# First feed-forward layer of a hybrid transformer block: weight blocks stationary, 256 token columns moving

## The chip, the cores and the metric

The kernel is one program on one core of a Trainium2 chip. The metric is the device time of the program in microseconds (us), the median of several executions. TensorE (PE in the profile) does the matrix products: it loads a stationary block of up to 128x128 values (a weight load, PEld in the profile) and streams the columns of a moving operand past it, up to 512 for one matmul, the width of one bank of PSUM in float32. PSUM has eight such banks. VectorE (DVE), ScalarE (ACT) and GpSimd (POOL) do the rest, and SyncE (SP) issues most of the loads.

## The reference

One block on 256 tokens of width 2048, all in float32: modulated RMS norm, a fused projection, grouped attention and a Fourier mixing branch, gates, an output projection with a residual, and then the part that matters here:

```python
def sq_relu_mlp(h, w1, w2):
    return jnp.square(jax.nn.relu(h @ w1)) @ w2

h2 = modulate(rmsnorm(x, norm2_g[l]), sh2, sc2)
x = x + g2 * sq_relu_mlp(h2, w1[l], w2[l])
```

`h2` is 256 x 2048, `w1` 2048 x 8192 and `w2` 8192 x 2048.

## The kernel before, in words

**Number format.** Every product is made of three. A float32 operand is split into a high part, the value rounded to float32r, and a low part, the rest. The product is high x high + high x low + low x high, three float32r matmuls that accumulate in PSUM (`products`, L1192 to L1198). Activations are kept as two tiles (`h2T[0]` high, `h2T[1]` low). Weights come as float32 tiles of 128 x 1024 (`raw`, eight slots, 512 KB each); ScalarE makes the high part in `wh` (`split_hi`, L583 to L588), VectorE the low part in `wl` (`split_lo`, L898 to L902). `wh` and `wl` have four slots each, and tile k takes slot k mod 4. ScalarE may write a slot when TensorE has finished the tile that was there (`gemm_done`); VectorE follows ScalarE (`wh_done`), TensorE follows VectorE (`wl_done`), and SyncE loads the next tile into `raw` when VectorE has read the slot.

**Order.** Each engine has a written-out order of its own. After the projections and attention the first feed-forward layer runs over eight blocks i of 1024 features and, in each, over sixteen tiles k of 128 rows of `w1` (`first_product`, L1414). For a tile, `tile_products` (L1200) goes over four banks: bank n holds tokens n mod 2 (128 of them, on partitions) by features n // 2 (512 of them, along columns). The stationary operand is the activation, `h2T[.][:, k, 128 tokens]`, the moving one 512 columns of the weights. So one tile is 4 x 3 = 12 matmuls of 512 columns with 12 weight loads, and all eight blocks use the same banks 0 to 3.

**Behind a block.** VectorE evicts the four banks with a relu into `hs`, tokens on partitions (`relu`, L1102, after the split of tile 1 of the next block). The second layer contracts over features and needs them on partitions, so TensorE transposes `hs` into banks 4 to 7 (`hidden_transposes`, L1421): four groups of four 128x128 transposes, after tiles 1 to 4 of the next block, or behind everything for the last block. ScalarE squares each of these banks into `hid` (`hidden`, L791, after its splits of tiles 3 to 6). `hid` holds all 8192 features by 256 tokens. The blocks 2 to 7 of TensorE are a hardware loop, those of the other engines 1 to 7.

**Around the layer.** In the first block, `xs_transposes` stand between the products: they bring the normalised activations features first, and ScalarE and VectorE make `h2T` from them while the first products run. The second layer (`second_product`, L1452) has the activations stationary again, as two tiles `hidS` that are cut from `hid` (L819 and L1150), and accumulates over all tiles in the eight banks; its tiles alternate between banks 0 to 3 and banks 4 to 7.

Of the kernel before, what the change touches and what calls it, by code (L numbers as in the profile page):

```python
# [21 lines left out]
F32 = mybir.dt.float32  # L22
# [5 lines left out]
P = 128  # L28
# [165 lines left out]
def block_program(nc, x, c, ctx_, c_ctx, w_ada, b_ada, norm1_g, w_in, q_norm_g, k_norm_g,  # L194
                  w_attn_o, w_fourier, w_out, norm2_g, w1, w2, final_norm_g,
                  identity, dft, rope_c, rope_s, out):
    with ExitStack() as stack:
# [10 lines left out]
        def place(name, shape, dt, region, skip=0):  # L208
            return nc.alloc_sbuf_tensor_at(name, shape, dt, offset=where[region] + skip)
# [26 lines left out]
        h2T = [place(f"h2T{i}", [P, KT, T], F32R, "h", i * 16384) for i in range(2)]  # L236
# [28 lines left out]
        hs = place("hs", [P, TB, NC], F32, "f")  # L265
# [65 lines left out]
        def sem(name):  # L331
            return stack.enter_context(nc.semaphore(name))
# [51 lines left out]
        x1_ready = sem("x1_ready")  # L384
        sq1_ready = sem("sq1_ready")
        xs_ready = sem("xs_ready")
        hT_full = sem("hT_full")
        hid_ready = sem("hid_ready")
        hs_hi = sem("hs_hi")
        hs_lo = sem("hs_lo")  # L390
# [170 lines left out]
        def _(act):  # L561
# [210 lines left out]
            def modulate2_hi(g):  # L772
                b = misc_wait_full(act, ("xs", g))
                for j in range(2):
                    f = 2 * g + j
                    nc.scalar.activation(h2T[0][:, f, :], b[:, j * T:(j + 1) * T], ACT.Identity,
                                         bias=mods2[:, 0, f:f + 1], scale=gain2[:, f:f + 1]).then_inc(hi_done, 1)

            for m, (name, k) in enumerate(TILES):
# [10 lines left out]

            def hidden(i, g):  # L791

                act.wait_ge(hT_full, i * 4 + (g + 1))
# [48 lines left out]
        def _(dve):  # L842
# [229 lines left out]
            def modulate2_lo(g):  # L1072
                b = misc_wait_full(dve, ("xs", g))

                dve.wait_ge(hi_done, HI_AT["xs", 2 * g + 1])
                if g >= 2:
                    misc_wait_freed(dve, ("xs", g - 2))
                for j in range(2):
                    f = 2 * g + j
                    then(nc.vector.tensor_scalar(hmod2[:, g % 2, j, :], b[:, j * T:(j + 1) * T], gain2[:, f:f + 1],  # L1080
                                                 mods2[:, 0, f:f + 1], ALU.mult, ALU.add))
                nc.vector.tensor_tensor(h2T[1][:, 2 * g:2 * g + 2, :], hmod2[:, g % 2, :, :],  # L1082
                                        h2T[0][:, 2 * g:2 * g + 2, :].bitcast(F32), ALU.subtract)\
                    .then_inc(misc_free[MISC_AT["xs", g][0]], 1)

            for m, (name, k) in enumerate(TILES):
# [12 lines left out]
            def lo_1(i, k):  # L1099
                split_lo(i * KT + (M1 + k + 1), S1 + k, wh[:, k % SPL, :], wl[:, k % SPL, :])  # L1100

            def relu(i):  # L1102

                for b in range(4):
                    if b < 3:
                        dve.wait_ge(bank_full, i * 3 + (3 * CI1 + b + 1))
                    else:
                        dve.wait_ge(gemm_done, i * KT + (M1 + KT))
                    if b == 0:

                        if not (isinstance(i, int) and i == 0):
                            dve.wait_ge(hT_full, i * 4)
                    nc.vector.tensor_scalar(hs[:, b % 2, b // 2 * HC:(b // 2 + 1) * HC], bank[b][:], 0.0, None, ALU.max)\
                        .then_inc(bank_free, 1)

            for k in range(KT):
                lo_1(0, k)
# [14 lines left out]
                if k in (10, 12):  # L1132
# [7 lines left out]
            with nc.vector.Fori(1, N1) as i:  # L1140
                for k in range(KT):
                    lo_1(i, k)
                    if k == 1:
                        relu(i - 1)

            def lo_2(g, j):
                if j % 4 == 0:
# [6 lines left out]
            for j in range(8):  # L1154
                lo_2(0, j)
                if j == 1:
                    relu(N1 - 1)
# [25 lines left out]
        def _(pe):  # L1183
# [227 lines left out]
                xs_transposes(g)  # L1411
            pe.wait_ge(bank_free, 4 * CI1)

            def first_product(i, k):  # L1414
                pe.wait_ge(wl_done, i * KT + (M1 + k + 1))
                if isinstance(i, int) and i == 0 and k % 2 == 0:
                    misc_wait_freed(pe, ("xs", k // 2))
                tile_products(h2T, k, k % SPL, range(4), k == 0, k == KT - 1,
                              i * 4 + (4 * CI1 - 3) if k == 0 else None)

            def hidden_transposes(i, g):  # L1421

                if g == 0:
                    pe.wait_ge(bank_free, i * 4 + 4 * (CI1 + 1))
                if isinstance(i, int) and i == 0:
                    if g in (1, 2, 3):
                        pe.wait_ge(misc_free[4 + g], _uses[4 + g])
                else:
                    pe.wait_ge(hid_ready, i * 4 + (g - 3))
                for n in range(4):  # L1430
                    f, t = 2 * g + n // 2, n % 2
                    ins = nc.tensor.transpose(bank[4 + g][:, n * P:(n + 1) * P], hs[:, t, f * P:(f + 1) * P], ident[:])  # L1432
                ins.then_inc(hT_full, 1)

            for k in range(KT):
                first_product(0, k)
                if XS_NOW + k < 8:
                    xs_transposes(XS_NOW + k)
            for k in range(KT):
                first_product(1, k)  # L1440
                if 1 <= k < 5:
                    hidden_transposes(0, k - 1)
            with nc.tensor.Fori(2, N1) as i:
                for k in range(KT):
                    first_product(i, k)
                    if 1 <= k < 5:
                        hidden_transposes(i - 1, k - 1)
            for g in range(4):
                hidden_transposes(N1 - 1, g)


            def second_product(g, j, start):  # L1452
                if j % 4 == 0:
                    pe.wait_ge(hs_lo, g * 2 + (j // 4 + 1))
                pe.wait_ge(wl_done, g * 8 + (M2 + j + 1))
                n = j % 2
                if start and j == 0:
                    pe.wait_ge(bank_free, 4 * (CI1 + N1))
                if start and j == 1:
                    pe.wait_ge(hid_ready, 4 * N1)  # L1460
                q, e = divmod(j // 2, 2)
                tile_products([hidS[0][:, q, :, :], hidS[1][:, q, :, :]], e, j % SPL, range(4 * n, 4 * n + 4),
                              start and j < 2, False)
# [70 lines left out]
```

## Time and profile before

| | |
|---|---|
| median of 3 runs | 1613.29 us (1612.23 to 1614.71) |
| span of the profiled execution, first to last instruction | 1612.2 us |
| TensorE matmul busy | 1552.2 us, 96% |
| VectorE busy | 989.5 us, 61% |
| ScalarE busy | 740.0 us, 46% |
| HBM read / written | 354.68 MB / 2.10 MB, 221 GB/s |
| granted TensorE clock, mean | 0.981 of full speed |

The profile is of one execution. Busy time counts a stretch in which at least one instruction of the engine runs. Matmuls are pipelined: the record of one is about as long as its latency, and the next starts before it ends, so the sum over records is more than the busy time. What a matmul costs in a full queue is the distance of two starts. The first product of the first feed-forward layer starts at 883.05 us, the first of the second at 1251.74.

### The profile page before, as it was taken

How to read it: one execution, taken by the hardware profiler on the slowest of the kernel's cores; microseconds unless marked ns; L12 is line 12 of the kernel's file. 1: busy time of each engine (PE TensorE's matmuls, PEld its weight loads, DVE VectorE, ACT ScalarE, POOL GpSimd, SP SyncE). 2: the span in 40 equal slices, each digit the busy share in tenths (PEclk: the TensorE clock that was granted, in tenths of full speed). 3: DMA queues.
4: the chain of work that ended last, by engine and by line, in shares of the span. 5: the costliest groups of instructions: out<-in, count | busy, mean ns of one | idle time of the engine just before them, and what ended most of it. 6: DMA issues, size and time to landing. Idle time of an engine off the chain costs nothing.

```text
span 1612.2 us, 19582 instructions
## 1 busy us (share of the span) xinstructions
PE 1552.2 (96%) x7009; PEld 1261.1 (78%) x7009; DVE 989.5 (61%) x1066; ACT 740.0 (46%) x1008; POOL 75.6 (5%) x70
## 2 busy tenths in 40 slices
PE   4898999999999999999998999999999999999997
PEld 3676887787788877878776888888888888888885
DVE  4776855387766666887886744444454545555556
ACT  5776433264454445433444544443434444444443
POOL 0334200010000000000000000000000000000001
PEclk8899999999999999999999999999999999999998
DMA  9777857577566667978985666556665555555552
GB/s 341 254 267 285 293 192 272 176 245 255 174 222 214 213 222 259 335 245 298 344 292 192 185 184 185 183 170 189 185 196 191 181 193 190 193 194 194 192 194 85
DMA packets 108100, 357.62 MB, mean 222 GB/s; under 512 B 10888, under 2 KB 11912, under 8 KB 106888
## 3 DMA queue, kind: packets, MB, share of 16 engines
q1 hardware_dynamic: 105984, 351.32, 65.1%
q10 hardware_dynamic: 2056, 5.51, 0.9%
q8 instruction: 38, 0.62, 0.2%
q14 instruction: 22, 0.18, 0.0%
HBM read 354.68 MB, written 2.10 MB: 221 GB/s over the span
## 4 chain that ended last, share of the span: by engine, by line
PE 83%; DVE 3%; ACT 2%; issue 1%; DMA 1%; POOL 0%; DVEq 0%; POOLq 0%; SPq 0%; ACTq 0%
PE bank L1195 25%; PE bank L1197 25%; PE bank L1196 25%; PE bank L1333 2%; PE bank L1315 1%; PE bank L1432 1%; PE bank L1286 1%; ACT wh L588 1%; PE bank L1273 1%; DVE wl L901 1%; PE bank L1323 1%; DMA raw<-in_w_fourier 1%; DMA raw<-in_w_out 1%; DVE acc L921 1%; PE bank L1251 1%
## 5 line engine op out<-in xcount | busy, mean ns | idle before, releaser
L901 DVE TENSOR_TENSOR wl<-raw,wh 128x1024 fp32r<-128x1024 f32 x508 | 616.4, 1224 | 514.6 <-ACT wh L588 514.0
L588 ACT ACTIVATE wh<-raw 128x1024 fp32r<-128x1024 f32 x508 | 530.8, 1058 | 472.3 <-PE bank L1197 447.5
L1195 PE MATMUL bank<-wh,hT 128*128 128x512 f32 x512 | 210.3, 411 | 0.0
L1195 PE MATMUL bank<-wh,h2T 128*128 128x512 f32 x512 | 203.3, 397 | 2.1 <-DVE h2T L1082 2.1
L1197 PE MATMUL bank<-wh,hT 128*128 128x512 f32 x512 | 200.9, 392 | 0.0
L1197 PE MATMUL bank<-wh,h2T 128*128 128x512 f32 x512 | 200.4, 391 | 0.0
L1196 PE MATMUL bank<-wl,hT 128*128 128x512 f32 x512 | 200.3, 391 | 0.0
L1196 PE MATMUL bank<-wl,h2T 128*128 128x512 f32 x512 | 200.1, 391 | 0.0
L1195 PE MATMUL bank<-wh,hidS 128*128 128x512 f32 x512 | 199.3, 389 | 0.0
L1197 PE MATMUL bank<-wh,hidS 128*128 128x512 f32 x512 | 199.2, 389 | 0.0
L1196 PE MATMUL bank<-wl,hidS 128*128 128x512 f32 x512 | 199.2, 389 | 0.0
L921 DVE SCALAR_TENSOR_TENSOR acc<-raw,cc,acc 128x1024 f32<-128x1024 f32 x120 | 153.4, 1279 | 0.3
L1195 PEld LDWEIGHTS bank<-wh,hT 128*128 128x128 f32 x512 | 97.1, 190 | 21.2 <-issue 2.8
L1196 PEld LDWEIGHTS bank<-wl,hT 128*128 128x128 f32 x512 | 97.0, 189 | 21.3 <-issue 2.4
L1195 PEld LDWEIGHTS bank<-wh,h2T 128*128 128x128 f32 x512 | 96.7, 189 | 21.5 <-issue 2.4
L1197 PEld LDWEIGHTS bank<-wh,hT 128*128 128x128 f32 x512 | 96.6, 189 | 21.5
L1197 PEld LDWEIGHTS bank<-wh,h2T 128*128 128x128 f32 x512 | 96.5, 189 | 20.6
L1197 PEld LDWEIGHTS bank<-wh,hidS 128*128 128x128 f32 x512 | 96.1, 188 | 20.1
L1196 PEld LDWEIGHTS bank<-wl,h2T 128*128 128x128 f32 x512 | 96.7, 189 | 19.3
L1196 PEld LDWEIGHTS bank<-wl,hidS 128*128 128x128 f32 x512 | 96.1, 188 | 19.9
L1195 PEld LDWEIGHTS bank<-wh,hidS 128*128 128x128 f32 x512 | 96.1, 188 | 19.8
L718 ACT ACTIVATE probs<-bank,nb,qs 128x512 f32<-128x512 f32 x32 | 24.9, 779 | 127.4 <-DVE nb L1014 127.4
(174 smaller groups left out, 1718.2 us busy)
## 6 DMA issues: line engine op xcount, KB each, us to landing
raw<-in_w SPq DMA_DIRECT2D x256, 512.0 KB, 4.3
raw<-in_w_ada SPq DMA_DIRECT2D x192, 512.0 KB, 5.1
raw<-in_w_in SPq DMA_DIRECT2D x128, 512.0 KB, 4.4
raw<-in_w_attn_o SPq DMA_DIRECT2D x32, 512.0 KB, 6.4
raw<-in_w_out SPq DMA_DIRECT2D x32, 512.0 KB, 6.6
raw<-in_w_fourier SPq DMA_DIRECT2D x16, 512.0 KB, 6.2
xt<-in_x ACTq DMA_DIRECT2D x2, 1024.0 KB, 9.5
ct<-in_ctx ACTq DMA_DIRECT2D x2, 1024.0 KB, 13.2
```

The lines of the kernel that those rows point to most:

```text
L588: nc.scalar.activation(slot, raw[:, s % RAW, :], ACT.Copy).then_inc(wh_done, 1)
L718: nc.scalar.activation(probs[:, u % 2, :], bank[4][:], ACT.Exp, bias=nb[:, u:u + 1], scale=qs[:, h // 8, col:col + 1], accum_out=rsum[:, u ...
L901: nc.vector.tensor_tensor(lo, raw[:, s % RAW, :], hi.bitcast(F32), ALU.subtract)\
L921: nc.vector.scalar_tensor_tensor(acc[:, jc % 2, :], raw[:, s % RAW, :], cc[:, k, 0:1], acc[:, jc % 2, :], ALU.mult, ALU.add).then_inc(mac_ ...
L1195: nc.tensor.matmul(bank[b][:], a_hi, w_hi, start=first, stop=False)
L1196: nc.tensor.matmul(bank[b][:], a_hi, w_lo, start=False, stop=False)
L1197: ins = nc.tensor.matmul(bank[b][:], a_lo, w_hi, start=False, stop=last)
L1251: ins = nc.tensor.matmul(b[:, f:f + 1], acc[:, jc % 2, f * P:(f + 1) * P], ones[:, 0:1], start=True, stop=True)
L1273: ins = nc.tensor.matmul(b[:], fin[:, t, d * P:(d + 1) * P], dft_sb[:, t, 0:2 * FG], start=(t == 0), stop=(t == TB - 1))
L1286: ins = nc.tensor.matmul(b[:, o * T:(o + 1) * T], dft_sb[:, e, tab + o * P:tab + (o + 1) * P], ab[:, 2 * g + e, part * T:(part + 1) * T], ...
L1315: nc.tensor.matmul(bank[4][:], qT[:, h, t * P:(t + 1) * P], kT[:, h // QPK, :], start=True, stop=True).then_inc(s_done, 1)
L1333: ins = nc.tensor.matmul(bank[7][:, 0:P], v[:, kb, h // QPK * HD:(h // QPK + 1) * HD], probsT[:, w % 2, kb, :], start=(kb == 0), stop=(kb ...
```

## The change

The weights become the stationary operand and the activations the moving one. For a tile k, the kernel goes over eight groups f of 128 features. Stationary is `wh[:, slot, 128 features]` or the same of `wl`, moving are all 256 tokens of `h2T`, high or low. The output has features on partitions and tokens along 256 columns; two groups f share a bank. So one tile is 8 x 3 = 24 matmuls of 256 columns with 24 weight loads. Since the output has features on partitions already, `hidden_transposes` goes away. VectorE's relu evicts a bank into `hs[:, b, :]` and ScalarE squares from there into `hid`. Blocks alternate between banks 0 to 3 and 4 to 7, so loops run over pairs of blocks. `h2T` becomes one tile with both parts, in the same place; `hs` keeps its place and size. The loads, the splits and the second layer's products stay as they are.

```diff
-                nc.scalar.activation(hid[:, bass.ds(i * 8 + 2 * g, 2), :], bank[4 + g][:].rearrange("p (f t) -> p f t", f=2),
+                nc.scalar.activation(hid[:, bass.ds(i * 8 + 2 * g, 2), :], hs[:, g, :].rearrange("p (f t) -> p f t", f=2),
                                      ACT.Square).then_inc(hid_ready, 1)
...
-            def relu(i):
+            def relu(pair, h):
                 for b in range(4):
...
-                    nc.vector.tensor_scalar(hs[:, b % 2, b // 2 * HC:(b // 2 + 1) * HC], bank[b][:], 0.0, None, ALU.max)\
-                        .then_inc(bank_free, 1)
+                    if not (isinstance(pair, int) and pair == 0 and h == 0):
+                        dve.wait_ge(hid_ready, pair * 8 + (4 * (h - 1) + b + 1))
+                    nc.vector.tensor_scalar(hs[:, b, :], bank[4 * h + b][:], 0.0, None, ALU.max).then_inc(relu_ready, 1)
...
-            def first_product(i, k):
-                pe.wait_ge(wl_done, i * KT + (M1 + k + 1))
...
-                tile_products(h2T, k, k % SPL, range(4), k == 0, k == KT - 1,
-                              i * 4 + (4 * CI1 - 3) if k == 0 else None)
-
-            def hidden_transposes(i, g):
...
-                for n in range(4):
-                    f, t = 2 * g + n // 2, n % 2
-                    ins = nc.tensor.transpose(bank[4 + g][:, n * P:(n + 1) * P], hs[:, t, f * P:(f + 1) * P], ident[:])
-                ins.then_inc(hT_full, 1)
+            def first_product(pair, h, k):
+                pe.wait_ge(wl_done, pair * (2 * KT) + (M1 + h * KT + k + 1))
...
+                elif k == 0:
+                    pe.wait_ge(relu_ready, pair * 8 + (4 * (h - 1)))
+                slot = k % SPL
+                for f in range(8):
+                    b, cols_f = bank[4 * h + f // 2], slice(f * P, (f + 1) * P)
+                    out_f = b[:, f % 2 * T:(f % 2 + 1) * T]
+                    nc.tensor.matmul(out_f, wl[:, slot, cols_f], h2T[:, 0, k, :], start=(k == 0 and f % 2 == 0), stop=False,
+                                     skip_group_check=True)
+                    nc.tensor.matmul(out_f, wh[:, slot, cols_f], h2T[:, 1, k, :], start=False, stop=False, skip_group_check=True)
+                    ins = nc.tensor.matmul(out_f, wh[:, slot, cols_f], h2T[:, 0, k, :], start=False, stop=(k == KT - 1),
+                                           skip_group_check=True)
+                    if f == 7:
+                        ins.then_inc(gemm_done, 1)
+                    elif k == KT - 1 and f % 2 == 1:
+                        ins.then_inc(bank_full, 1)
...
             def second_product(g, j, start):
...
-                if start and j == 0:
-                    pe.wait_ge(bank_free, 4 * (CI1 + N1))
-                if start and j == 1:
-                    pe.wait_ge(hid_ready, 4 * N1)
+                if start and j < 2:
+                    pe.wait_ge(relu_ready, 4 * (N1 - 1 + j))
```

## Rows read from the trace of the kernel before

**Rows 1.** The page: busy share of TensorE, and the chain by engine.

```profile
PE 1552.2 (96%) x7009; PEld 1261.1 (78%) x7009; DVE 989.5 (61%) x1066; ACT 740.0 (46%) x1008; POOL 75.6 (5%) x70
...
PE 83%; DVE 3%; ACT 2%; issue 1%; DMA 1%; POOL 0%; DVEq 0%; POOLq 0%; SPq 0%; ACTq 0%
```

**Rows 2.** Busy time by stretch: length, each engine, granted clock, DMA share, GB/s.

```profile
936.35:981.80 45.45, 45.45 (x209) 37.61 (x208) 21.88 (x20) 18.80 (x20) 0.00 (x0) 1.00 0.61 185
...
1163.60:1209.05 45.45, 45.45 (x209) 37.62 (x208) 21.88 (x20) 18.80 (x20) 0.00 (x0) 1.00 0.61 184
```

**Rows 3.** Groups of instructions, 883 to 1252 us: busy us, mean ns | idle before.

```profile
L1195 PE MATMUL bank<-wh,h2T 128*128 128x512 f32 x512 | 203.3, 397 | 2.1 <-DVE h2T L1082 2.1
...
L901 DVE TENSOR_TENSOR wl<-raw,wh 128x1024 fp32r<-128x1024 f32 x128 | 154.7, 1223 | 164.6 <-ACT wh L588 164.6
L588 ACT ACTIVATE wh<-raw 128x1024 fp32r<-128x1024 f32 x128 | 134.6, 1058 | 130.0 <-PE bank L1197 130.0
L1195 PEld LDWEIGHTS bank<-wh,h2T 128*128 128x128 f32 x512 | 96.7, 189 | 21.5 <-issue 2.4
...
L1432 PE MATMUL bank<-ident,hs 128*128 128x128 f32 x128 | 18.7, 272 | 0.8 <-DVE hs L1113 0.8
```

**Rows 4.** Waits, 883 to 1252 us: us in total, times, longest.

```profile
DVE wl L901 <- ACT wh L588: 164.6, 92, 4.6
ACT wh L588 <- PE bank L1197: 130.0, 85, 1.7
```

**Rows 5.** Timeline of matmuls inside a block: start, us, instruction.

```profile
1000.05 0.39 PE L1195 MATMUL bank<-wh,h2T 128*128 128x512 f32 x1
...
1001.41 0.39 PE L1195 MATMUL bank<-wh,h2T 128*128 128x512 f32 x1
```

**Rows 6.** Timeline: groups of transposes in a block, and the next block's first.

```profile
936.35 0.60 PE L1432 MATMUL bank<-ident,hs 128*128 128x128 f32 x4
...
939.56 0.60 PE L1432 MATMUL bank<-ident,hs 128*128 128x128 f32 x4
...
981.80 0.60 PE L1432 MATMUL bank<-ident,hs 128*128 128x128 f32 x4
```

**Rows 7.** Timeline of all engines at the end of the layer.

```profile
1247.23 2.73 DVE L1113 TENSOR_SCALAR hs<-bank 128x512 f32<-128x512 f32 x4 [1.02 <-PE bank L1197]
...
1248.85 0.39 PE L1197 MATMUL bank<-wh,h2T 128*128 128x512 f32 x1
1250.02 1.96 PE L1432 MATMUL bank<-ident,hs 128*128 128x128 f32 x16 [0.79 <-DVE hs L1113]
1250.71 2.06 ACT L794 ACTIVATE hid<-bank 128x512 f32<-128x512 f32 x4 [5.76 <-PE bank L1432]
1251.74 0.48 PE L1195 MATMUL bank<-wh,hidS 128*128 128x512 f32 x1
```

**Rows 8.** Timeline of weight loads at the start of the second layer.

```profile
1251.71 0.19 PEld L1195 LDWEIGHTS bank<-wh,hidS 128*128 128x128 f32 x1
1251.83 0.19 PEld L1196 LDWEIGHTS bank<-wl,hidS 128*128 128x128 f32 x1
```

**Rows 9.** Timeline in attention: eight short float32 matmuls and their loads.

```profile
502.69 1.06 PE L1333 MATMUL bank<-probsT,v 128*128 128x128 f32 x8
...
502.58 0.97 PEld L1333 LDWEIGHTS bank<-probsT,v 128*128 128x128 f32 x8
```

**Rows 10.** Groups of instructions over the span: float32 matmuls of three sizes.

```profile
L1333 PE MATMUL bank<-probsT,v 128*128 128x128 f32 x256 | 34.1, 277 | 0.0
...
L1286 PE MATMUL bank<-ab,dft_sb 128*128 128x256 f32 x64 | 14.5, 379 | 0.0
...
L1408 PE MATMUL bank<-acc,ones 128*128 128x512 f32 x8 | 3.6, 592 | 0.0
```

**Rows 11.** Timeline: float32 matmuls of 256 and of 512 columns in a row.

```profile
306.42 2.75 PE L1286 MATMUL bank<-ab,dft_sb 128*128 128x256 f32 x12
...
872.96 3.59 PE L1408 MATMUL bank<-acc,ones 128*128 128x512 f32 x8
```

More of the change, by code:

```diff
@@ L235, in block_program @@
         mT = [place(f"mT{i}", [P, KT, T], F32R, "h", i * 16384) for i in range(2)]
-        h2T = [place(f"h2T{i}", [P, KT, T], F32R, "h", i * 16384) for i in range(2)]
+        h2T = place("h2T", [P, 2, KT, T], F32R, "h")
         yT = [place(f"yT{i}", [P, FW // P, T], F32R, "f", i * 8192) for i in range(2)]
@@ L264, in block_program @@
         xs = place("xs", [P, TB, D], F32, "x")
-        hs = place("hs", [P, TB, NC], F32, "f")
+        hs = place("hs", [P, 4, HC], F32, "f")
         hmod2 = place("hmod2", [P, 2, 2, T], F32, "f", 8192)
@@ L1081, in modulate2_lo @@
                                                  mods2[:, 0, f:f + 1], ALU.mult, ALU.add))
-                nc.vector.tensor_tensor(h2T[1][:, 2 * g:2 * g + 2, :], hmod2[:, g % 2, :, :],
-                                        h2T[0][:, 2 * g:2 * g + 2, :].bitcast(F32), ALU.subtract)\
+                nc.vector.tensor_tensor(h2T[:, 1, 2 * g:2 * g + 2, :], hmod2[:, g % 2, :, :],
+                                        h2T[:, 0, 2 * g:2 * g + 2, :].bitcast(F32), ALU.subtract)\
                     .then_inc(misc_free[MISC_AT["xs", g][0]], 1)
@@ L1100, in lo_1 @@
                 split_lo(i * KT + (M1 + k + 1), S1 + k, wh[:, k % SPL, :], wl[:, k % SPL, :])
[L1102 removed]
+            def relu(pair, h):
                 for b in range(4):
                     if b < 3:
[L1106 removed]
+                        dve.wait_ge(bank_full, pair * 6 + (3 * (CI1 + h) + b + 1))
                     else:
[L1108 to L1112, printed above, removed]
[L1113 to L1114 removed]
+                        dve.wait_ge(gemm_done, pair * (2 * KT) + (M1 + (h + 1) * KT))
+                    if not (isinstance(pair, int) and pair == 0 and h == 0):
+                        dve.wait_ge(hid_ready, pair * 8 + (4 * (h - 1) + b + 1))
+                    nc.vector.tensor_scalar(hs[:, b, :], bank[4 * h + b][:], 0.0, None, ALU.max).then_inc(relu_ready, 1)
             for k in range(KT):
@@ L1139, in _ @@
                     then(nc.vector.tensor_tensor(part, part, acc[:, half, :], ALU.add))
[L1140 to L1144, printed above, removed]
+            for k in range(KT):
+                lo_1(1, k)
+                if k == 1:
+                    relu(0, 0)
+            with nc.vector.Fori(1, N1 // 2) as pair:
+                for h in range(2):
+                    for k in range(KT):
+                        lo_1(pair * 2 + h, k)
+                        if k == 1:
+                            relu(pair - 1 + h, 1 - h)
             def lo_2(g, j):
@@ L1156, in _ @@
                 if j == 1:
-                    relu(N1 - 1)
+                    relu(N1 // 2 - 1, 1)
             with nc.vector.Fori(1, N2 // 8) as g:
@@ L1412, in _ @@
             pe.wait_ge(bank_free, 4 * CI1)
-            def first_product(i, k):
-                pe.wait_ge(wl_done, i * KT + (M1 + k + 1))
-                if isinstance(i, int) and i == 0 and k % 2 == 0:
-                    misc_wait_freed(pe, ("xs", k // 2))
-                tile_products(h2T, k, k % SPL, range(4), k == 0, k == KT - 1,
-                              i * 4 + (4 * CI1 - 3) if k == 0 else None)
-            def hidden_transposes(i, g):
[L1423 to L1429, printed above, removed]
-                for n in range(4):
-                    f, t = 2 * g + n // 2, n % 2
-                    ins = nc.tensor.transpose(bank[4 + g][:, n * P:(n + 1) * P], hs[:, t, f * P:(f + 1) * P], ident[:])
-                ins.then_inc(hT_full, 1)
+            def first_product(pair, h, k):
+                pe.wait_ge(wl_done, pair * (2 * KT) + (M1 + h * KT + k + 1))
+                if isinstance(pair, int) and pair == 0:
+                    if h == 0 and k % 2 == 0:
+                        misc_wait_freed(pe, ("xs", k // 2))
+                    if h == 1 and k == 0:
+                        for b in (5, 6, 7):
+                            pe.wait_ge(misc_free[b], _uses[b])
+                elif k == 0:
[13 more added lines that the diff above has]
+                        ins.then_inc(bank_full, 1)
@@ L1439, in _ @@
             for k in range(KT):
[L1440 to L1449, printed above, removed]
+                first_product(0, 1, k)
+            with nc.tensor.Fori(1, N1 // 2) as pair:
+                for h in range(2):
+                    for k in range(KT):
+                        first_product(pair, h, k)
             def second_product(g, j, start):
```

8 lines of the change are left out of this document (4 added, 4 removed).

## The prediction

> **What bounds the kernel now.** I read the page's busy shares and its chain first: TensorE is busy for 96% of the 1612.2 us and holds 83% of the chain that ended last [rows 1]. So the time is the sum of TensorE's own work, and an edit pays only by what it takes from or adds to that queue. Then the busy time by block: each of the six middle blocks of the first feed-forward layer (there are eight; the first and the last of the six are shown) takes 45.45 us, TensorE is busy in all of it, and the granted clock is 1.00, the upper of the two levels (2.4 GHz) [rows 2]. A block is 16 weight tiles (k) of 12 matmuls of 512 columns, and four groups of four transposes. The groups of instructions and the waits of this stage say who has room: VectorE spends 1223 ns and ScalarE 1058 ns on a tile, and both of them wait, VectorE for ScalarE and ScalarE for TensorE, 164.6 and 130.0 us in all [rows 3, 4]. The stage is TensorE's alone.
>
> The timeline of matmuls gives the pace: starts at 1000.05 and 1001.41, six matmuls apart, so 226.7 ns for one of 512 columns in float32r [rows 5]. The 389 ns or so of one record [rows 3] is its latency, not its cost. A tile is 12 x 0.2267 = 2.72 us, sixteen are 43.52, and 45.45 - 43.52 = 1.93 us is what the transposes of a block cost. The other way round: groups of transposes start 3.21 us apart (936.35, 939.56) with one tile between them, and 3.21 - 2.72 = 0.49 each; the same group of the next block starts at 981.80, 45.45 later [rows 6].
>
> **What the change removes.** (a) The 16 transposes of a block: 1.93 us in each of the seven blocks whose transposes stand between products, 13.5 us. (b) The last block's transposes stand alone at the end. The last product of the layer starts at 1248.85; then TensorE waits for the last relu, transposes from 1250.02 and the next layer's first record starts at 1251.74 [rows 7]. That product really runs from 1251.83, when the weight load after its own starts [rows 8] (a load starts with the matmul ahead of it). That is 2.98 us where 0.23 would do: 2.75 us. Together 16.3 us.
>
> **What it adds.** Each matmul of 512 columns becomes two of 256, each behind a weight load of its own: 1536 become 3072, 24 in a tile, and the columns streamed are the same. All hangs on the pace x of such a pair of load and matmul; before, 1536 x 0.2267 = 348.2 us, after, 3072 times x. No float32r matmul of 256 columns is in the trace, so x is bounded by neighbours.
>
> From below, the weight load. It is 188 or 189 ns long as a record [rows 3], but loads follow each other faster: after the transposes two float32r loads start at 1251.71 and 1251.83, some 0.11 apart [rows 8]. In attention eight loads with eight short float32 matmuls take 0.97 us with 0.19 for the last: (0.97 - 0.19)/7 = 0.111, and their matmuls, with 277 ns for one, (1.06 - 0.277)/7 = 0.112 [rows 9, 10]. So x is at least 0.112: 344.1 us, 4.1 less than now.
>
> From above. That a load is not hidden at all, 0.11 + 0.113 us a pair and some 340 us more for the layer, is excluded by the same rows and by rows 5, where a load starts with the matmul ahead of it. What is left is the fixed part of a matmul. 512 columns at 2.4 GHz are 213.3 ns, so 13.3 ns of the 226.7 are something else. If they belong to each matmul whatever its size, x is 106.7 + 13.3 = 120.0 ns: 368.6 us, 20.4 more. If they go with the columns (the stream runs at 16/17 of the clock), x is 113.3 and nothing changes. The float32 matmuls say how a stretch divides: 12 of 256 columns take 2.75 us with 379 ns for the last, (2.75 - 0.379)/11 = 0.2155 each, and 8 of 512 take 3.59, (3.59 - 0.592)/7 = 0.428 [rows 10, 11]. Two of 256 cost 431 ns for 428, so what is fixed is about 3 ns per matmul, not 13. That row is the nearest, since it changes exactly the size in question. With 0 to 3 ns fixed in 226.7, x is 113.3 to 114.9; I take 113.8: 349.6 us, 1.4 more than now. The sum: -16.3 + 1.4 = -14.9 us.
>
> A third bound is the issue of instructions, twice as many per tile. From 1250.02, after a wait of 0.79 us in which the queue stood, 16 pairs of load and transpose take 1.96 us with 0.272 for the last, 0.1125 a pair [rows 3, 7]; no row shows it kept up for longer than 16 pairs. The Trainium skill, "TensorE: Matmul & The Clock Gate", section "What happens when you issue a matmul", gives about 62 ns per MATMUL when the sequencer's own code handles it. If a weight load cost the same, a pair would take 124 ns, the layer 381 us, and the change would be slower by about 16 us. By that rule the trace disagrees, 0.1125 for 0.124, as far as it goes.
>
> **The edits with one answer.** Relu moves from a wait of TensorE to none: the layer now uses banks 0 to 3 and 4 to 7 by turns, so a product waits for relus of a block before the last, which ended some 40 us earlier. VectorE does the same four evictions of about 0.69 us in the same place, now into a tile that ScalarE squares from SBUF instead of from a bank; both instructions stay off the path, and if the square were twice as long (about 0.6 us more, four times a block), ScalarE's 130 us of waiting cover it [rows 4]. VectorE's relu gains a wait for a square that was done about ten tiles earlier: queued behind it are the splits of the next tiles, and nothing makes it late. One h2T tile in place of two, no loads moved, no DMA added or moved past a queue, the SP queue unchanged: nothing. PSUM accumulates three times into the same 256 columns at 0.114 us; in attention eight records in a row accumulate into the same 128 columns at 0.112 without a stall [rows 9]. The first block keeps its eight groups of x transposes and its start at the lower clock, where as many columns are streamed as before: nothing.
>
> **What is late next at the hand-over.** The second layer's first product could start at 1249.08. It needs the split of its tile, done before the relus that start at 1247.23, and banks 0 to 3, long free. The second (at 1251.8) needs banks 4 to 7: the last relu ends at 1247.23 + 2.73 = 1249.96 [rows 7]. The third (at 1254.5) needs the split behind the four squares: these follow the relus, 0.6 us each, and end near 1250.6; one ScalarE copy (1.06) and one VectorE subtraction (1.22) later it is about 1252.9, 1.6 us early. So the 2.75 us of (b) are won in full.
>
> **The rivals.** (A) The fixed cost. The 13.3 ns are paid by every matmul, or by every weight load beside a float32r stream, which comes to the same. Then the change loses 20.4 and wins 16.3: slower by 4.1 us, 1617.4. For it: float32r is the only kind here that has these 13 ns, every one has a load beside it, and the float32 matmuls stream at half its rate, so rows 11 cannot speak for a limit of that kind. Against it: a limit on the rate of the stream explains as well why float32 is spared. It decides from x = 348.2 + 16.3 = 364.5 us over 3072, that is 118.7 ns. (B) Part of it: load and stream hinder each other and x lands between 115.5 and 118.7, which gives from 1603.6 to no gain at all. (C) The weight load alone is the bound, x = 0.112: -4.1 - 16.3 = -20.4, 1592.9. For it speak rows 9; against it, the stream of 256 columns would have to run faster than any in rows 5. The same skill page, "Back-to-back issue gap", has N/2.4 + 2.5 ns: 109.2 for 256 columns. By that figure the layer would take 335.5 us and the change would win 29; the measured 226.7 for 512 where it has 215.8 says that it does not hold for this kernel's kind. (D) Issue or instruction fetch cannot keep 48 records in a tile of 2.7 us and x is above 121: over 1620. Against it speaks the pace of the 16 pairs [rows 7], for it only that nothing longer is shown. (E) The change works, but something I have not seen holds the gain at the hand-over or in the loops: within 0.2%.
>
> **How the numbers follow.** The profiled execution spans 1612.2 us, 1.1 below the median of 1613.3, so I subtract from the median: 1613.3 - 14.9 = 1598.4. Chances: the forecast (x of 112.8 to 115.5, 1595.3 to 1603.6) 0.57; (C) 0.08; (B) 0.11; (A) 0.14; (D) 0.07; (E) 0.03. A measurement of this kernel can tell 0.2%, 3.2 us. Faster by more than that are the forecast, (C) and most of (B): 0.73. Slower are (A) and (D), 0.21, and a little of (B). The same: what is left of (B), and (E), 0.05. The range goes from 1592 to 1618, which leaves out (D) and a little at the low end; the likeliest case's own range is 1595 to 1604.
>
> **What would show it.** Right: the products of the first layer at 256 columns with records of about 283 ns (389 less the 107 of the other half) and six starts 0.68 us apart; no transposes of hs; blocks of 16 x 2.73 = 43.7 us; the first product of the second layer within 0.3 us of the last one of the first; ScalarE and VectorE still waiting for TensorE. Wrong in the way of (A): the same picture with blocks of 46.1 us. (D) would show as idle time of the weight loads put down to issue. A granted clock below 1.00 in the layer would overthrow all of it, and so would a wait of TensorE for splits at the head of a block.

## The result, and the profile after

The changed kernel takes 1615.42 us (median of 20 runs, 1611.83 to 1618.52), the kernel before 1611.4 in 20 runs of its own (1608.33 to 1614.71). The ratio is 1.0025, 95% interval 1.0015 to 1.0034: slower by 4.0 us. Single executions of each kernel spread over some 6.5 us, but lowest lies 3.5 and highest 3.8 us above the other's. The forecast was 1598.4; what came is rival (A), which said slower by 4.1.

The page shows little of the cause: TensorE is as busy and holds as much of the chain as before [rows 1], and only the weight loads' share has grown, from 78% to 82%:

```profile
PE 1554.4 (96%) x8417; PEld 1328.3 (82%) x8417; DVE 991.9 (61%) x1066; ACT 742.0 (46%) x1008; POOL 75.6 (5%) x70
...
PE 83%; DVE 3%; ACT 2%; issue 1%; DMA 1%; POOL 0%; DVEq 0%; POOLq 0%; SPq 0%; ACTq 0%
```

Busy time by stretch, for two blocks in the middle (columns as in [rows 2]). A block is 46.08 us, 16 tiles of 2.88, where it was 45.45. The weight loads, busy for 37.6 us of a block before, now fill it. The granted clock is still 1.00:

```profile
936.35:982.45 46.10, 46.10 (x386) 46.10 (x386) 22.19 (x20) 19.04 (x21) 0.00 (x0) 1.00 0.60 183
1163.60:1209.70 46.10, 46.10 (x387) 46.10 (x386) 22.24 (x21) 19.03 (x21) 0.00 (x0) 1.00 0.60 182
```

The groups of instructions of the layer, as [rows 3]: the record of a matmul is 284 ns, about what was expected, which shows again that a record is no pace; the load's has grown from 189 to 193, and its idle time has gone from 21.5 us to none.

```profile
L1434 PE MATMUL bank<-h2T,wh 128*128 128x256 f32 x1024 | 291.3, 284 | 0.0
...
L1434 PEld LDWEIGHTS bank<-h2T,wh 128*128 128x128 f32 x1023 | 197.6, 193 | 0.0
...
L901 DVE TENSOR_TENSOR wl<-raw,wh 128x1024 fp32r<-128x1024 f32 x128 | 155.9, 1224 | 166.6 <-ACT wh L588 166.6
L588 ACT ACTIVATE wh<-raw 128x1024 fp32r<-128x1024 f32 x127 | 134.3, 1058 | 203.5 <-PE bank L1435 203.5
...
L794 ACT ACTIVATE hid<-hs 128x512 f32 x28 | 17.2, 615 | 0.0
```

The timeline of matmuls, as [rows 5], has the number on which the sum hung. These two stand 18 matmuls apart, so x = 2.16 / 18 = 120.0 ns:

```profile
999.76 0.28 PE L1432 MATMUL bank<-h2T,wl 128*128 128x256 f32 x1
...
1001.92 0.28 PE L1432 MATMUL bank<-h2T,wl 128*128 128x256 f32 x1
```

And the hand-over, as [rows 7]: the second layer starts 0.12 us after the last product of the first (1254.88), while VectorE's relus and ScalarE's squares run behind it.

```profile
1253.04 2.85 DVE L1112 TENSOR_SCALAR hs<-bank 128x512 f32<-128x512 f32 x4 [1.22 <-PE bank L1435]
1253.77 2.79 ACT L794 ACTIVATE hid<-hs 128x512 f32<-128x512 f32 x4 [3.20 <-DVE hs L1112]
1255.00 0.40 PE L1198 MATMUL bank<-wh,hidS 128*128 128x512 f32 x1
```

From its first product to the first of the second layer, the layer took 1251.74 - 883.05 = 368.69 us before and 1255.00 - 882.24 = 372.76 after: +4.07. That is the whole difference. Both have a stretch at the lower clock (granted 0.50) at the start of the layer, 3.9 us of it before and 4.3 after, which costs either about 1.9 us and so explains none of it (columns as in [rows 2], before and after):

```profile
883.05:887.00 3.95, 3.95 (x10) 3.11 (x10) 3.81 (x7) 0.53 (x1) 0.00 (x0) 0.51 0.00 0
```

```profile
882.24:886.50 4.26, 4.26 (x20) 4.26 (x21) 4.12 (x7) 0.64 (x1) 0.00 (x0) 0.50 0.00 0
```

### The profile page after: what moved, and what is told of

It reads as the page before. It is cut to its first block, busy times and chain, and to the rows that moved or that the text cites. A ratio compares the mean times of both kernels' runs of the same rounds, so it can differ in the third digit from the quotient of the medians.

```text
span 1615.4 us, 22341 instructions
## 1 busy us (share of the span) xinstructions
PE 1554.4 (96%) x8417; PEld 1328.3 (82%) x8417; DVE 991.9 (61%) x1066; ACT 742.0 (46%) x1008; POOL 75.6 (5%) x70
## 4 chain that ended last, share of the span: by engine, by line
PE 83%; DVE 3%; ACT 2%; issue 1%; DMA 1%; POOL 0%; DVEq 0%; POOLq 0%; SPq 0%; ACTq 0%
PE bank L1198 18%; PE bank L1200 18%; PE bank L1199 18%; PE bank L1432 8%; PE bank L1434 8%; PE bank L1435 8%; PE bank L1336 2%; PE bank L1318 1%; PE bank L1289 1%; ACT wh L588 1%; PE bank L1276 1%; DVE wl L901 1%; PE bank L1326 1%; DMA raw<-in_w_out 1%; DVE acc L921 1%
## 5 line engine op out<-in xcount | busy, mean ns | idle before, releaser
L1432 PE MATMUL bank<-h2T,wl 128*128 128x256 f32 x1024 | 291.8, 285 | 2.2 <-DVE h2T L1082 2.2
L1434 PE MATMUL bank<-h2T,wh 128*128 128x256 f32 x1024 | 291.3, 284 | 0.0
L1435 PE MATMUL bank<-h2T,wh 128*128 128x256 f32 x1024 | 291.2, 284 | 0.0
L1432 PEld LDWEIGHTS bank<-h2T,wl 128*128 128x128 f32 x1024 | 198.0, 193 | 2.5 <-issue 2.5
L1434 PEld LDWEIGHTS bank<-h2T,wh 128*128 128x128 f32 x1024 | 198.0, 193 | 0.0
L1435 PEld LDWEIGHTS bank<-h2T,wh 128*128 128x128 f32 x1024 | 197.8, 193 | 0.0
```

The source lines that it names most:

```text
L1432: nc.tensor.matmul(out_f, wl[:, slot, cols_f], h2T[:, 0, k, :], start=(k == 0 and f % 2 == 0), stop=False, skip_group_check=True)
L1434: nc.tensor.matmul(out_f, wh[:, slot, cols_f], h2T[:, 1, k, :], start=False, stop=False, skip_group_check=True)
L1435: ins = nc.tensor.matmul(out_f, wh[:, slot, cols_f], h2T[:, 0, k, :], start=False, stop=(k == KT - 1), skip_group_check=True)
```

## The experiments

Runs a to d, f, h, i, k and l were executed once. Single executions of one kernel lie some 6 us apart, so their spans tell only larger differences; what is compared is the distance of starts in the first layer, at the upper clock. Over a long even stretch it repeats (226.67 ns in the kernel before and in e, 230.0 in h and k). "Excess" is that distance less columns / 2.4 GHz. Theories as they stood in the expectations: 1, every float32r matmul pays 13.3 ns; 2, the weight load beside the stream costs it; 3, the load of 128 columns is itself 120 ns long and binds.

**a: half the weight columns.** The other half of the features is left out.

```diff
-                    b, cols_f = bank[4 * h + f // 2], slice(f * P, (f + 1) * P)
+                    b, cols_f = bank[4 * h + f // 2], slice(f * P, f * P + P // 2)
```

> The changed kernel, but each matmul of the first layer loads only the first 64 of its 128 weight columns (half of the features are left out), moving columns still 256. Theory 1 (13.3 ns are paid by every float32r matmul, whatever it loads): starts still 120.0 ns apart, span as after, 1615 us. Theory 2 (the 13.3 ns come from the weight load that runs beside the stream): the load is half as long and so is the cost, 113.3 ns, span 1615.4 - 3072 x 0.0067 = 1595 us. Theory 3 (a float32r weight load of 128 columns takes 120 ns and is what sets the pace): the load no longer binds, the stream does, 107 to 113 ns, span 1575 to 1595 us.

Measured: span 1590.8 us. The timeline, two starts 24 matmuls apart, 2.71 / 24 = 113 ns (113.33 over a longer stretch), and the groups:

```profile
999.82 0.28 PE L1432 MATMUL bank<-h2T,wl 128*64 128x256 f32 x1
...
1002.53 0.28 PE L1432 MATMUL bank<-h2T,wl 128*64 128x256 f32 x1
```

```profile
L1434 PE MATMUL bank<-h2T,wh 128*64 128x256 f32 x969 | 267.5, 276 | 0.0
...
L1434 PEld LDWEIGHTS bank<-h2T,wh 128*64 128x64 f32 x968 | 129.7, 134 | 0.0
```

Half a load, half the excess (6.7 ns), at the same 256 columns. Theory 1 falls: the cost is not of the matmul as such. Nor can the load set 113 ns, since c has the same half loads 60 ns apart; so here the stream itself is slower than its columns. (Half a load is also half the rows of output; the two can't be parted here.)

**b: half the moving columns.** Half of the tokens is left out.

```diff
-                    ... h2T[:, 0, k, :] ...
+                    ... h2T[:, 0, k, 0:P] ...
```

> The changed kernel, but each matmul of the first layer moves 128 columns, half of the tokens (the others are left out), with full loads of 128 weight columns. Theory 1: the stream would take 53.3 + 13.3 = 66.7 ns, so the weight load binds at the 112 ns of the attention's float32 pairs: layer 344 us, span 1591 us. Theory 2: the load runs beside the stream all the time, 112 to 120 ns. Theory 3: still 120.0 ns, span 1615 us. The tiles still take 1.06 + 1.22 us of ScalarE and VectorE, less than a tile of 24 x 0.112 = 2.7 us.

Measured: span 1898.5 us, which no theory had. The reason is the clock. At first, at the upper level (2.4 GHz), starts are (880.95 - 879.28) / 15 = 111.3 ns apart; at 881 the distance goes to 213, and the granted clock stays at 0.50 (1.2 GHz) until the layer ends at 1536. The timeline, and the busy time by stretch with the granted clock third from the end:

```profile
879.28 0.27 PE L1435 MATMUL bank<-h2T,wh 128*128 128x128 f32 x1
...
880.95 0.28 PE L1435 MATMUL bank<-h2T,wh 128*128 128x128 f32 x1
881.06 0.34 PE L1432 MATMUL bank<-h2T,wl 128*128 128x128 f32 x1
881.20 0.41 PE L1434 MATMUL bank<-h2T,wh 128*128 128x128 f32 x1
881.42 0.41 PE L1435 MATMUL bank<-h2T,wh 128*128 128x128 f32 x1
```

```profile
900.00:920.00 20.00, 20.00 (x96) 20.00 (x96) 9.98 (x12) 6.99 (x9) 0.00 (x0) 0.50 0.45 132
...
1400.00:1440.00 40.00, 40.00 (x190) 40.00 (x189) 9.23 (x8) 8.10 (x8) 0.00 (x0) 0.50 0.37 105
```

Of the question asked, the first 1.7 us answer it: a float32r load of 128 columns with a short stream beside it needs 111 to 112 ns, not 120. Theory 3 is in trouble.

**c: half of both.**

```diff
+                    ... slice(f * P, f * P + P // 2) ... b[0:P // 2, f % 2 * T:f % 2 * T + P] ... h2T[:, 0, k, 0:P]
```

> The changed kernel with 64 weight columns loaded and 128 columns moved in each matmul of the first layer (three quarters of its work left out). Theory 1: 53.3 + 13.3 = 66.7 ns per matmul, 24 in 1.6 us. Theory 2: 53.3 + 6.7 = 60.0. Theory 3: 60.0 as well (half of 120). A tile of 1.4 to 1.6 us is close to VectorE's 1.22 us and to loads of 512 KB at some 3 us, so TensorE may wait at tiles: only the distance of starts inside a tile is to be read, not the span.

Measured: single starts 57 to 63 ns apart; 16 matmuls in 0.96 us are 60.0, excess 6.7, the number of theories 2 and 3, with TensorE waiting some 6 us in all for splits:

```profile
999.78 0.22 PE L1432 MATMUL bank<-h2T,wl 128*64 128x128 f32 x1
...
1000.74 0.22 PE L1434 MATMUL bank<-h2T,wh 128*64 128x128 f32 x1
```

It excludes 66.7 and so theory 1 once more, and parts nothing else. The granted clock was 0.50 at the start of the layer here too, but came back to 1.00 before 887 and stayed, with the same 128 columns moved as in b.

**d: only the cut.** The kernel before, each matmul of 512 columns in two of 256.

```diff
+                        for e in range(2):
+                            w_cols = slice(half * HC + e * T, half * HC + (e + 1) * T)
+                            ins = nc.tensor.matmul(bank[n][:, e * T:(e + 1) * T], a[act_part][:, k, cols_t], w_part[:, slot, w_cols], ...
```

> The kernel before, with activations stationary and all transposes, but each matmul of 512 columns of the first layer cut into two of 256, each with its own load of the same 128 columns. If the price is that of the number of matmuls alone (theories 1 to 3 agree): starts 120.0 ns apart, layer 20.5 us longer, span 1612.2 + 20.5 = 1632.7 us. If it is tied to which operand stands and which moves, or a load of a block that already stands is cheaper: less, down to 113.3 ns and 1612 us.

Measured: span 1631.3 us, starts 120.0 ns apart, layer 387.39 us, 18.7 more than before. Which operand stands and which moves makes no difference, and the second load of a block that already stands costs as much as the first. (20.5 had been reckoned for the layer. The same group of transposes starts at 939.22 and again at 987.03, a block of 47.81 us; less 384 x 0.12 the transposes of a block cost 1.73 us here and not 1.93, 1.4 us less over seven blocks.)

**e: only the removal.** The kernel before without its transposes.

```diff
-                act.wait_ge(hT_full, i * 4 + (g + 1))
-                nc.scalar.activation(hid[...], bank[4 + g][:]...
+                act.wait_ge(bank_free, i * 4 + (4 * CI1 + g + 1))
+                nc.scalar.activation(hid[...], hs[:, g % 2, g // 2 * HC:(g // 2 + 1) * HC]...
...
-                    if 1 <= k < 5:
-                        hidden_transposes(i - 1, k - 1)
```

> The kernel before without the transposes of hs (they are left out, ScalarE squares the untransposed relu). My accounting of what the change removes: 13.5 us between products and at the end 2.98 us less the wait for the last relu that stays, some 1.17: 15.3 us less than before, ratio 0.9905. If the removal had been worth less than reckoned (the change's loss would then be no matter of the loads): 1600 us or more.

Measured: ratio 0.9901 (0.9878 to 0.9924), some 16 us; the layer takes 1233.56 - 880.24 = 353.32 us, 15.4 less. The wait for the last relu, reckoned at 1.17 us from start to start, is 1233.56 - 1232.29 = 1.27:

```profile
1232.29 0.39 PE L1198 MATMUL bank<-wh,h2T 128*128 128x512 f32 x1
1233.56 0.47 PE L1196 MATMUL bank<-wh,hidS 128*128 128x512 f32 x1 [0.88 <-DVE hs L1114]
```

So the two halves of the change were also run apart: the cut alone costs 18.7 us (d), the removal alone brings 15.4 (e), together +3.3 for the +4.07 of both at once.

**f: the changed kernel with the layer's parts in bfloat16** (less accurate).

```diff
-        h2T = place("h2T", [P, 2, KT, T], F32R, "h")
+        h2T = place("h2T", [P, 2, KT, T], BF16, "h")
+        whb = place("whb", [P, SPL, 2 * NC], BF16, "wh")
+        wlb = place("wlb", [P, SPL, 2 * NC], BF16, "wl")
```

> The changed kernel with the parts of the first layer in bfloat16 instead of float32r (less accurate, same count and shape of matmuls and loads). If the 13.3 ns of a load come from two 4-byte streams meeting (stationary and moving operand read at once): with half the bytes nothing or a small rest remains, 107 to 110 ns a pair, span 1615.4 - 3072 x 0.011 = 1581 us. If a load costs 32 clocks of the array whatever it reads: 120 ns and 1615 us. If the load itself is shorter in bfloat16 its record will be below 192 ns, and the cost may fall with it.

Measured: span 1580.9 us. 24 matmuls in 2.62 us are 109.2 ns, excess 2.5. The record of a matmul is 273 ns, not 284, that of a load 98, not 193:

```profile
999.76 0.27 PE L1437 MATMUL bank<-h2T,wlb 128*128 128x256 bf16 x1
...
1002.38 0.27 PE L1437 MATMUL bank<-h2T,wlb 128*128 128x256 bf16 x1
```

```profile
L1439 PE MATMUL bank<-h2T,whb 128*128 128x256 bf16 x1005 | 273.9, 273 | 0.0
...
L1437 PEld LDWEIGHTS bank<-h2T,wlb 128*128 128x128 bf16 x1004 | 98.2, 98 | 11.3
```

**l: the kernel before in bfloat16**, the same edit.

> The kernel before, with the parts of the first layer in bfloat16 (less accurate; matmuls of 512 columns, transposes as before). If the 13.3 ns are float32r's alone: 213.3 + 2.5 = 215.8 ns a matmul, layer 16.7 us shorter, span 1595 us; the changed kernel in bfloat16, 1580.9, is then faster than this by about 14 us, what the transposes and the hand-over cost less two or three for the loads: in bfloat16 the change would pay. If 512 columns keep the excess: 226.7 and 1612 us.

Measured: span 1589.7 us. 12 matmuls of 512 columns in 2.59 us are 215.8 ns, excess 2.5 as well:

```profile
999.75 0.38 PE L1201 MATMUL bank<-wlb,h2T 128*128 128x512 bf16 x1
...
1002.34 0.38 PE L1201 MATMUL bank<-wlb,h2T 128*128 128x512 bf16 x1
```

The layer takes 348.59 us here and 339.48 in f: in bfloat16 the very same change gains 9.1 us as the traces stand, where in float32r it loses 4.1. The two are not at the same clock: f has 4.2 us at granted 0.50 at the start of its layer and l has none. By an estimate from the starts (20 matmuls 213 ns apart there, 109 later) that costs f about 2 us, so at one clock the gain is about 11, less than the 14 that I had written down. Granted clock, third from the end, at the start of the layer, f and then l:

```profile
880.93:885.00 4.07, 4.07 (x20) 2.81 (x21) 3.93 (x7) 0.63 (x1) 0.00 (x0) 0.50 0.00 0
```

```profile
880.55:885.00 4.45, 4.45 (x23) 2.32 (x24) 4.31 (x8) 1.75 (x4) 0.00 (x0) 1.00 0.00 0
```

**h and k: half the stationary columns at 512 moving columns.** The kernel before, half of the tokens left out; k takes the other half of each 128.

```diff
-                    cols_t = slice(t * P, (t + 1) * P)
+                    cols_t = slice(t * P, t * P + P // 2)          # h
+                    cols_t = slice(t * P + P // 2, (t + 1) * P)    # k
```

> The kernel before, but each matmul of the first layer loads only 64 of its 128 activation columns (half of the tokens are left out), moving 512 columns of weights. If the cost is of the load beside the stream, 13.3 ns for 128 weight columns and 6.7 for 64 whatever is moved: 213.3 + 6.7 = 220.0 ns, layer 10.2 us shorter, 1602 us. If it goes with the columns moved at 512 after all, or is of the matmul: 226.7 ns, 1612 us.

> As the run before with half loads of activations and 512 moving columns, but the loads take columns 64 to 127 of each 128 instead of 0 to 63, 256 bytes further on. There the distance of starts was 230.0 ns on average and went through 229, 225, 226, 226, 234, 230 over and over, not 220.0. If the excess depends on where stationary and moving operand lie relative to each other: another order of distances or another mean. If it is of the size alone: the same 230.0 and the same order.

Measured: 12 matmuls of h in 2.76 us, 230 ns each, spans 1613.5 and 1611.3 us. I had expected 220.0; half a load makes the distance at 512 columns longer, not shorter. Single distances go through 229, 225, 226, 234, 230, 236 ns over and over (the order in the expectation of k is misread and would not give 230 on average). k repeats both the 230.0 and this order, so it does not hang on these 256 bytes.

```profile
999.72 0.63 PE L1423 MATMUL bank<-wh,h2T 128*64 128x512 f32 x2
...
1002.48 0.63 PE L1423 MATMUL bank<-wh,h2T 128*64 128x512 f32 x2
```

**i: three quarters of the moving columns**, a quarter of the tokens left out (`h2T[:, 0, k, 0:192]`).

> The changed kernel with 192 of the 256 tokens moved (64 are left out) and full loads. If at 256 the stream sets the pace and a load beside it costs it 13.3 ns: 80 + 13.3 = 93 ns is less than the 112 of loads alone, so starts are 112 ns apart. If the load is what binds at 256 and takes 120 ns beside a float32r stream: still 120, or a little less for the part in which no stream runs, 115 to 120. With 112 the layer is 24.6 us shorter, 1591 us. The granted clock fell to 0.50 with 128 columns; if it does here as well, starts are 213 ns apart.

Measured: span 1586.1 us, 24 matmuls in 2.68 us, 111.7 ns each, with the clock at 1.00 and the load's record at 192:

```profile
999.75 0.27 PE L1435 MATMUL bank<-h2T,wh 128*128 128x192 f32 x1
...
1002.43 0.27 PE L1435 MATMUL bank<-h2T,wh 128*128 128x192 f32 x1
```

Theory 3 falls: with a stream of 80 ns beside it the load needs 111.7, and 120 at 256 columns is not its own length. The starts of the loads say the same. Here a load starts at 1000.11, after the matmul ahead of it (1000.09); in the changed kernel, at 1000.12, together with it (1000.12). In i the loads set the pace, and at 256 columns they wait for the stream. First i, then the changed kernel:

```profile
1000.09 0.28 PE L1435 MATMUL bank<-h2T,wh 128*128 128x192 f32 x1
1000.11 0.19 PEld L1432 LDWEIGHTS bank<-h2T,wl 128*128 128x128 f32 x1
```

```profile
1000.12 0.28 PE L1432 MATMUL bank<-h2T,wl 128*128 128x256 f32 x1
1000.12 0.19 PEld L1434 LDWEIGHTS bank<-h2T,wh 128*128 128x128 f32 x1
```

**g and m: a version for both.** The high part of a weight block moves the high and the low tokens at once, 512 columns; the low part moves the high tokens, 256. Two loads for 768 columns instead of three. VectorE adds the two halves of a bank, ScalarE does relu and square, and tiles are two rows by 512 features so that blocks still alternate between four banks and four.

```diff
+                        nc.tensor.matmul(b[:].rearrange("p (a t) -> p a t", a=2), wh[:, slot, cols_f], h2T[:, :, kk, :],
+                                         start=(kk == 0), stop=False, skip_group_check=True)
+                        ins = nc.tensor.matmul(b[:, 0:T], wl[:, slot, cols_f], h2T[:, 0, kk, :], start=False, stop=last,
+                                               skip_group_check=True)
...
+                    nc.vector.tensor_reduce(hs[:, b, 0:T], bank[4 * t + b][:].rearrange("p (a t) -> p t a", a=2), AX.X,
+                                            ALU.add).then_inc(relu_ready, 1)
```

> A version meant to beat both: weight blocks stationary as in the changed kernel, but the high part of a weight block moves the high and the low tokens in one matmul of 512 columns and the low part moves the high tokens, 256: two loads for 768 columns instead of three. A block of features needs a whole bank then (its two halves are added by VectorE, ScalarE does relu and square), so a weight tile is two rows of 512 features and blocks of 512 features use banks 0 to 3 and 4 to 7 by turns. If a load of 128 columns costs 13.3 ns (what the half loads showed; a cost per matmul would give the same here): 226.7 + 120.0 = 346.7 ns for one block of 128 features and one k, a tile of 8 is 2.77 us, the layer 355.0 us against 348.2 before and 368.6 after; with 16.3 us of transposes and hand-over saved 9.5 us faster than before, ratio 0.994. If the cost were tied to moving from the halves of one tile or to evictions that read a bank with a step, slower than that by what VectorE's evictions take beyond 0.69 us each, hidden as long as TensorE waits for nothing.

Measured: ratio 0.9942 (0.9920 to 0.9964). The timeline has 9 pairs in 3.18 us, 353 ns a pair and not 346.7:

```profile
999.71 0.40 PE L1445 MATMUL bank<-h2T,wh 128*128 128x512 f32 x1
...
1002.89 0.40 PE L1445 MATMUL bank<-h2T,wh 128*128 128x512 f32 x1
```

The layer takes 1243.51 - 879.55 = 363.96 us, 4.7 less than before. About 1.9 of these are the clock: g has no stretch at 0.50 at the start of the layer. The other 2.8 are about what pairs of 353.3 ns leave of the 9.5 reckoned (1024 x 6.6 ns = 6.8 less). The ratio says 9.4 (5.8 to 12.9); the profiled execution is one of the slower of its kernel (1606.26 us in all, median 1602.12). Why others are up to 7 us faster is not shown.

m does for one k the four matmuls of 512 first and then the four of 256:

> The version with two matmuls a product, in another order: for one k first the four matmuls of 512 columns (high weights, high and low tokens), then the four of 256 (low weights, high tokens). In the first order, 512 and 256 by turns, a pair took 352.4 ns, not 346.7: some 116.6 from a 512 start to... the 256 part and 236 the other, and the layer 364 us against 369 before. If the excess beside a load depends on what stands next to what (runs of equal size showed 226.7 and 120.0 exactly): 346.7 again, layer 1024 x 5.7 ns = 5.8 us shorter, 358 us, ratio against the kernel before some 0.991 to 0.993. If it depends on moving both parts of the token tile at once: 352.4 as before and 0.994 to 0.997.

Measured: ratio 0.9958 (0.9946 to 0.9971), the layer 361.39 us, 7.3 less than before (1.9 of it again the clock) and 2.6 less than g. A pair took 350.8 ns on average between 950 and 1200 us, where g took 353.3. So neither of the two answers: the order matters little, and the excess stays at 15 to 17 ns per matmul where it was 13.3 in streams of one size. Both versions beat the kernel before by about half a per cent; their intervals overlap, and neither ran beside the changed kernel.

## Why the prediction was wrong, point by point

**What bounds the kernel**: right. TensorE is the bound before and after.

**What is removed** (13.5 + 2.75 = 16.3 us): right. e, which keeps the wait for the last relu, measured 15.4 us for the 15.3 reckoned for it, and that wait 1.27 for 1.17. In the change the hand-over is 0.12 us, its last product 1254.88, the next 1255.00.

**The edits with one answer, and what is late next**: right. VectorE's relus still wait for TensorE only, TensorE waits for nothing in the blocks, and the splits of the second layer come in time. The start at the lower clock costs both kernels the same, about 1.9 us. (Loads that start with the matmul ahead of them are not in rows 5, where the text finds them, but the trace has them: matmul and load both at 1000.05.)

**What is added**: wrong, and this is the step. The text took x = 113.8 ns, +1.4 us, and gave as reason that two float32 matmuls of 256 columns cost 431 ns for one of 428, "the nearest, since it changes exactly the size in question". x is 120.0: 3072 x 0.120 - 348.2 = +20.4 us, and 20.4 - 16.3 = +4.1 for the measured +4.07 in the trace of the layer. The row changed the right size in the wrong format. It was also misread: a float32 matmul leaves two records (L1408 issues four matmuls and has eight records), so 428 and 215.5 ns are the pace of a record, and a float32 matmul of 512 columns takes 856 ns, a quarter of float32r's rate, with two loads. For the forecast that changes nothing, since two matmuls of 256 columns still cost only 862 ns (4 x 215.5) for one of 856. bfloat16 streams at float32r's rate and has 2.5 ns of excess at 256 and at 512 columns (f, l), float32r has 13.3 at both (before, after, d). So a stream at one column per clock is not the cause by itself. What float32r has alone here is four bytes a column at that rate.

**Whose cost it is.** The runs put it on the stream, while a load runs beside it, as far as they go. At 256 columns half a load halves it (a: 113.3), and at 128 columns half a load has the same 6.7 (c). The load isn't the binding one (i: 111.7 with 192 columns, b: 111.3 with 128), and its record stays at 192 to 193 ns in i, after and the start of b, while the matmul's goes from 273 ns (f) to 276 (a) to 284 (after). And the cost is there at the upper clock only. In the changed kernel's stretch at 0.50, the same loads stand beside the same streams, and 12 matmuls take 2.56 us, 213.3 ns each, which is 256 columns at 1.2 GHz with no excess at all:

```profile
883.66 0.42 PE L1432 MATMUL bank<-h2T,wl 128*128 128x256 f32 x1
...
886.22 0.41 PE L1432 MATMUL bank<-h2T,wl 128*128 128x256 f32 x1
```

The Trainium skill, "TensorE: Matmul & The Clock Gate", section "What happens when you issue a matmul", says that the two operands have read ports of their own and that loading the next block takes no read bandwidth from the running matmul. In bfloat16 nothing speaks against it (2.5 ns of excess); in float32r at 256 columns the runs do, 120.0 ns with a full load and 113.3 with half of one, at the upper clock. That the meeting of two reads of four bytes is the mechanism is what I think, and no run shows it: there is none with a float32r matmul that has no load beside it, and half a load was always half the rows of output too.

**What stays open.** At 512 columns half a load does not halve the excess: it goes from 13.3 to 16.7 ns (h), whichever half is loaded (k). This speaks against any account in which the cost simply grows with the load, the one above too. Even streams of full loads keep one distance, where half loads at 512 columns go through 224 to 236 ns (h, k) and the 512-column matmuls of mixed streams through 224 to 241 (g, m). So 13.3 ns per load is the measured price for full loads at 256 and 512 columns in streams of one size, no law for others.

**The rivals.** (A) came, with its number. Its first form, a price of every matmul whatever it loads, falls with a; its second, of every load beside a float32r stream, stands at 256 columns. The text had even said why rows 11 cannot speak for float32r; it had 0.14. The weakness was in the weighing: a caveat that takes away the only row for the forecast should have moved the chance, and 0.57 stayed on it. (B), (C) and (D) are excluded: 24 pairs in 2.88 us, 48 records, are kept up for the whole layer with no idle time of TensorE in the blocks. (C)'s bound of 0.112 is real, as i shows, and just not reached at 256 columns. The sentence in which 226.7 ns were put down to a stream that runs at 16/17 of the clock was a possibility for one size only, and the forecast was built on it.

## What to carry to other kernels

Count the weight loads of a float32r kernel, not only the columns: each load of 128 columns beside the stream cost 13.3 ns here, 12.5% of 106.7 at 256 moving columns and 6% of 213.3 at 512, so a transposition saved by swapping the operands must pay for the loads it doubles. Where the same stationary block is used for two operands (high and low parts), let one matmul move both: two loads for three made the swap pay, by about half a per cent. And a row in another format is no nearest neighbour for the fixed part of a cost, even when it changes just the size in question; in bfloat16 the same change gained 9.1 us, an estimated 11 at one clock. Before two traces are compared to a few us, look at the granted clock of both, stretch by stretch.

## What the runs showed of the hardware that I had not expected

- In eight of the traces (before, after, b, c, d, e, f, h) the granted clock goes to 0.50 at the start of the layer, where TensorE has just waited, and in all of these but b it is back at 1.00 within 7 us. In the other six (a, g, i, k, l, m) it stays at 1.00, although TensorE waits there as well. Which of the two an execution gets is not explained here.
- With 128 moving columns and loads of 128 it did not come back until the layer ended, some 655 us later, though neither matmuls nor loads were ever idle (b: starts 213 ns apart, span 1898.5). With the same 128 columns and half loads it did, from starts 107 ns apart to 60 (c). With 192 columns at 111.7 ns it never fell, so i does not show whether it would have come back. Moving fewer columns made the kernel slower by 283 us.
- At granted 0.50 the 13.3 ns are gone: 213.3 ns for 256 columns with a full load, where 120.0 at 1.00 is more than half of that.
- A bfloat16 load has a record of 98 ns, a float32r one of 188 to 193 (128 columns) or 134 (64 columns).
- A second load of the block that already stands costs as much as any (d: 120.0 ns throughout).
